# 32-column inverses in a chunked recurrence, its output normalised in the last head pair, and an output projection begun over them

## The reference, cut to what matters

```
def step(state, inp):                       # 256 steps, 16 heads of 64
    r_t, w_t, k_t, v_t, a_t, b_t = inp
    sa = einsum('bhvk,bhk->bhv', state, a_t)
    state = state * w_t + sa * b_t + v_t * k_t
    y_t = einsum('bhvk,bhk->bhv', state, r_t)
mean, var = mean(y), mean((y - mean)^2)     # over the 64 of a head
y = (y - mean) * rsqrt(var + 64e-5) * lnx_w + lnx_b
y = (y + sum(r * k * r_k) * v) * g
x = x + y @ w_o
```

## Time and profile before

| | us |
|---|---|
| median of 3 runs | 1403.82 (1401.42 to 1408.97) |
| the profiled execution's own time | 1402.62 |
| its span in the trace | 1400.4 |
| scores, projection of r, levels and steps of pair 0 to 3 | 99.3 to 322.4 |
| normalisation and output projection | 322.4 to 365.8 |

### The profile page before, as it was taken

One profiled execution on the slowest core, in us unless ns is written; L12 is line 12 of the kernel. 1 busy time (PEld: TensorE's weight loads), 2 busy tenths in 40 slices (PEclk: granted clock), 3 DMA queues, 4 the chain that ended last, 5 costly groups with the idle time before them and its releaser, 6 DMA issues.

```text
span 1400.4 us, 21886 instructions
## 1 busy us (share of the span) xinstructions
PE 1255.3 (90%) x9218; PEld 1167.3 (83%) x9218; DVE 940.1 (67%) x1298; ACT 630.4 (45%) x829; POOL 208.5 (15%) x139
## 2 busy tenths in 40 slices
PE   3998989887899999699888889999789887999995
PEld 3887878775899999696667888999789877999995
DVE  6767657544468874755864567774548835999994
ACT  4464343224443445456556564434442244544442
POOL 0000000000264442000000122210000001344431
PEclk9999999898999999899998999999899997999998
DMA  7440001000577764253322668785342213545530
GB/s 269 151 154 31 32 1 61 1 1 1 196 268 246 247 214 154 90 184 117 119 92 95 216 246 286 268 288 181 121 151 91 90 61 120 175 164 185 186 135 30
DMA packets 122656, 200.20 MB, mean 143 GB/s; under 512 B 3264, under 2 KB 111168, under 8 KB 112320
## 3 DMA queue, kind: packets, MB, share of 16 engines
q1 hardware_dynamic: 117664, 168.05, 35.7%
q0 software_dynamic: 3456, 25.17, 4.8%
q10 hardware_dynamic: 1440, 5.60, 1.1%
HBM read 197.75 MB, written 1.05 MB: 142 GB/s over the span
## 4 chain that ended last, share of the span: by engine, by line
PE 63%; DVE 24%; ACT 7%; issue 5%; DMA 0%; DVEq 0%; POOL 0%; ACTq 0%
PE bank L631 13%; PE bank L632 12%; PE bank L633 12%; DVE buf L2390 7%; DVE ring_r L1696 6%; PE bank L714 3%; PE bank L716 3%; PE bank L715 3%; ACT high L1173 2%; DVE work L1952 2%; PE bank L647 2%; PE bank L869 2%; DVE work L1948 2%; PE bank L857 2%; PE bank L1065 1%
## 5 line engine op out<-in xcount | busy, mean ns | idle before, releaser
L631 PE MATMUL bank<-part,high 128*128 128x256 f32 x1664 | 485.8, 292 | 66.6 <-DVE part L1703 61.5
L632 PE MATMUL bank<-part,high 128*128 128x256 f32 x1664 | 481.7, 289 | 0.0
L1696 DVE TENSOR_TENSOR ring_r<-ring,high 128x2048 fp32r<-128x2048 f32 (+1 forms) x155 | 342.9, 2221 | 206.3 <-ACT high L1173 204.0
L633 PE MATMUL bank<-part,ring_r 128*128 128x256 f32 x1664 | 481.1, 289 | 0.0
L631 PEld LDWEIGHTS bank<-part,high 128*128 128x128 f32 x1664 | 329.4, 198 | 75.3 <-issue 52.6
L632 PEld LDWEIGHTS bank<-part,high 128*128 128x128 f32 x1664 | 329.5, 198 | 0.3 <-issue 0.2
L633 PEld LDWEIGHTS bank<-part,ring_r 128*128 128x128 f32 x1664 | 329.1, 198 | 0.0
L1173 ACT ACTIVATE high<-ring 128x2048 fp32r<-128x2048 f32 x155 | 295.2, 1906 | 51.1 <-PE bank L633 40.9
L1623 POOL TENSOR_TENSOR ring_r<-ring,high 128x512 fp32r<-128x512 f32 x44 | 95.4, 2167 | 534.0 <-ACT high L1173 533.9
L714 PE MATMUL bank<-part,high 128*128 128x256 f32 x528 | 151.3, 287 | 9.2 <-POOL part L1617 4.9
L715 PE MATMUL bank<-part,high 128*128 128x256 f32 x528 | 150.1, 284 | 0.0
(11 more groups left out here) (260 smaller groups left out, 1580.9 us busy)
## 6 DMA issues: line engine op xcount, KB each, us to landing
ring<-in_wide SPq DMA_DIRECT2D x122, 1024.0 KB, 5.9
ring<-in_down SPq DMA_DIRECT2D x33, 1024.0 KB, 5.0
buf<-in_wide POOLq DMA_DIRECT2D x24, 1024.0 KB, 7.2
con<-in_cons SPq DMA_DIRECT2D x1, 1472.0 KB, 10.9
ring<-in_wide SPq DMA_DIRECT2D x2, 576.0 KB, 7.0
buf<-in_wide ACTq DMA_DIRECT2D x1, 1024.0 KB, 5.4
buf<-in_wide SPq DMA_DIRECT2D x1, 1024.0 KB, 5.3
buf<-in_ctx_t ACTq DMA_DIRECT2D x1, 1024.0 KB, 4.7
```

Source lines behind the costliest of these rows:

```text
L631: mm(bank, ah, bh, start=start, stop=False, skip_group_check=shared)
L632: mm(bank, ah, bl, start=False, stop=False, skip_group_check=shared)
L633: return mm(bank, al, bh, start=False, stop=stop, skip_group_check=shared)
L1696: v.tensor_tensor(low, raw, hi.bitcast(F32), ALU.subtract).then_inc(sem("unit_low"), 1)
```

## The change

**Levels 1 to 4** work on the blocks of the diagonal only. X of four 32x32 blocks is kept as a tile of 128 partitions by 32 columns (`x`, for four systems 128x128), and y and dx move 32 columns instead of 128, with a stationary matrix of 128x128 still: `near` (the scores inside the diagonal blocks) for y and the block-diagonal `xt` for dx. y now reads X as it is and dx reads it transposed, so the next y waits for the predicated copy alone (`x_ready`), and dx for the transposes (`xt_ready`). The transposes are four of 32x128 in place of one of 128x512. **Level 5** uses `far` (the scores between diagonal blocks, two small ScalarE copies of each group at level 1); its dx is eight matmuls in place of four, with 64 and 96 stationary columns, and TensorE's transposes at level 5 are gone. Small ScalarE copies (`left_diagonal`, `left_corner`) and two VectorE transposes build the operands of level 6. **Scores:** a fifth, small matmul in each of the 8 banks. **Setup of a pair:** VectorE has one more operation of 128x512 (`near`) and three more transposes for a group. **Pair 3:** ahead of its levels TensorE subtracts the mean of quarters 0 to 2 by one matmul each (`y_centre`), ScalarE squares and copies them, TensorE sums the squares after level 1, the Ln and Exp stand between the levels, and VectorE's operations for quarters 0 to 2 (`y_out`) stand before `st` and after it. **Projection:** TensorE does the first six of eight row tiles of units 0, 1 and 2, then the last two of each, then unit 3. The table of constants is 512 columns longer.

```diff
-        y_sq = buf[11]
+        y_sq = buf[1]
+        def chain_parts(g):
+
+            t = work[:, g % 2]
+            return t[:, 0, :], t[:, 1, :], t[:, 2, :], t[:, 3, 0:P], t[:, 3, P:2 * P]
+        def left_of(g):
+
+            return work[0:CH, g % 2, 3, 2 * P:4 * P].rearrange("p (j n) -> p j n", j=4)
...
+                def y_centre(j):
+                    for g in (2 * j, 2 * j + 1):
+                        wait_freed(pe, ("yt", g))
+                    bank = open_bank(("yc", j))
+                    close(mm(bank[:, :], const("centre"), piece(y_t, j), start=True, stop=True), ("yc", j))
+
+                def y_variance(j):
+                    pe.wait_ge(sem("y_sq"), j + 1)
+                    bank = open_bank(("yvar", j))
+                    close(mm(bank[:, :], const("head_sum"), piece(y_sq, j), start=True, stop=True), ("yvar", j))
+                def o_tiles(i, kts):
+                    w = arrived("o", i // 2, i % 2)
+                    bank = bank_of(("o", i)) if kts[0] else open_bank(("o", i))
+                    for kt in kts:
+                        wait_part("y", kt)
+                        for half in range(2):
+                            last = split_mm(bank[:, half * S:(half + 1) * S], [z[:, kt, half * P:(half + 1) * P] for z in w], tile_of("y", kt),
+                                            kt + half == 0, kt == KT - 1, shared=True)
+                    if kts[-1] == KT - 1:
+                        close(last, ("o", i))
...
-                                mm(bank[:, 0:P], at_, bt_, start=True, stop=True)
+                                mm(bank[:, 0:P], bt_, at_, start=True, stop=True)
+                                mm(bank[CH:P, 0:CH], at_[:, CH:P], bt_[:, 0:CH], start=True, stop=True)
...
+                    else:
+                        for j in range(p):
+                            y_centre(j)
...
-                                pe.wait_ge(sem(f"xt_ready{g % 2}"), SQUARE * (g // 2) + l)
+                                pe.wait_ge(sem(f"x_ready{g % 2}"), SQUARE * (g // 2) + l)
+                            if l == SQUARE:
+                                pe.wait_ge(sem(f"far_ready{g % 2}"), g // 2 + 1)
-                                    last = mm(bank[:, s_], scores[g % 2][:, j, 0:P], xt[:, s_], start=True, stop=True)
+                                    last = mm(bank[:, j * SQ:(j + 1) * SQ], (near if l < SQUARE else far)[:, s_], x[:, j * SQ:(j + 1) * SQ], start=True, stop=True)
...
+                            if l <= SQUARE:
+                                pe.wait_ge(sem(f"xt_ready{g % 2}"), SQUARE * (g // 2) + l)
+                            else:
+                                pe.wait_ge(sem(f"x_left{g % 2}"), g // 2 + 1)
                             for j in range(4):
-                                s_ = slice(j * P, (j + 1) * P)
-                                if what == "dx":
-                                    last = mm(bank[:, s_], y[:, s_], x[:, s_], start=True, stop=True)
+                                y_ = y[:, j * SQ:(j + 1) * SQ]
+                                if l < SQUARE:
+                                    last = mm(bank[:, j * SQ:(j + 1) * SQ], xt[:, j * P:(j + 1) * P], y_, start=True, stop=True)
+                                elif what == "dx":
+                                    mm(bank[0:CH, (4 + j) * SQ:(5 + j) * SQ], xt[:, j * P:j * P + CH], y_, start=True, stop=True)
+                                    last = mm(bank[0:P - SQ, j * SQ:(j + 1) * SQ], xt[:, j * P + SQ:(j + 1) * P], y_, start=True, stop=True)
                                 else:
-                                    last = mm(bank[0:CH, j * CH:(j + 1) * CH], x[0:CH, j * P:j * P + CH], y[0:CH, j * CH:(j + 1) * CH], start=True, stop=True)
+                                    last = mm(bank[0:CH, j * CH:(j + 1) * CH], left_of(g)[:, j, :], wide_y(g)[:, j * CH:(j + 1) * CH], start=True, stop=True)
...
-                                    s_ = slice(j * P, (j + 1) * P)
-                                    last = nc.tensor.transpose(bank[:, s_], x[:, s_], ident)
+                        elif l == 1:
+                            for j in range(p):
+                                y_variance(j)
...
-                for g in range(NG):
-                    wait_freed(pe, ("yt", g))
-                sums_over("ymean", const("head_sum"), y_t, lambda j: None)
-                sums_over("yvar", const("head_sum"), y_sq, lambda j: pe.wait_ge(sem("y_sq"), j + 1))
-                project("o", "y")
+                y_centre(3)
+                o_tiles(0, range(0, 6))
+                y_variance(3)
+                for i in (1, 2):
+                    o_tiles(i, range(0, 6))
+                for i in range(3):
+                    o_tiles(i, range(6, KT))
+                o_tiles(3, range(0, KT))
...
+                    far = squares(chain_parts(g)[1])
+                    own.go(act_(far[0:SQ, :, SQ:CH], scores[g % 2][0:SQ, :, SQ:CH], ACT.Copy))
+                    act_(far[CH:CH + SQ, :, CH + SQ:P], scores[g % 2][CH:CH + SQ, :, CH + SQ:P], ACT.Copy).then_inc(sem(f"far_ready{g % 2}"), 1)
...
+                    for b in range(2):
+                        r = slice(b * SQ, (b + 1) * SQ)
+                        own.go(act_(left_of(g)[r, :, r], x[r, :, :], ACT.Copy))
...
+                    act_(left_of(g)[SQ:CH, :, 0:SQ], bank_of(key)[SQ:CH, P:2 * P].rearrange("p (j n) -> p j n", j=4), ACT.Copy).then_inc(sem(f"x_left{g % 2}"), 1)
...
+                    wait_full(eng, key)
+                    act_(piece(y_sq, j), bank_of(key)[:, :], ACT.Square).then_inc(sem("y_sq"), 1)
+                    release(act_(piece(y_t, j), bank_of(key)[:, :], ACT.Copy), key)
...
+                            y_square(j)
+                        log_table()
...
-                            m, n = (P, 512) if l < LEV - 1 else (CH, 4 * CH)
-                            release(act_(work[0:m, g % 2, 3, 0:n], bank_of(key)[0:m, 0:n], ACT.Copy), key)
-                        if SQUARE <= l < LEV - 1:
+                            if l < LEV - 1:
+                                release(act_(chain_parts(g)[3], bank_of(key)[:, 0:P], ACT.Copy), key)
+                            else:
+                                release(act_(wide_y(g), bank_of(key)[0:CH, 0:4 * CH], ACT.Copy), key)
-                                release(act_(work[:, g % 2, 2, :], bank_of(key)[:, :], ACT.Copy), key)
+                                far_blocks(g)
+                        if l == SQUARE:
+                            for g in pair:
+                                left_diagonal(g)
+                            own.settle()
+                            for g in pair:
+                                left_corner(g)
...
+                        elif l <= 3:
+                            y_log(l - 1)
+                        else:
+                            y_root(l - 4)
...
+                        if not nxt and what in ("sa0", "sa1"):
+                            part_of("y", what == "sa1")
...
-                for j in range(4):
-                    eng.wait_ge(sem("y_centered"), j + 1)
-                    act_(piece(y_sq, j), piece(y_t, j), ACT.Square).then_inc(sem("y_sq"), 1)
-                rsqrt_of([(("yvar", j), piece(y_sq, j)) for j in range(4)], CH, eps_lnx, "y_root")
-                parts("y")
+                log_table()
+                y_square(3)
+                part_of("y", 2)
+                y_log(3)
+                y_root(3)
+                part_of("y", 3)
...
+                    def turned(g, back):
+
+                        xt, x = squares(chain_parts(g)[2]), squares(chain_parts(g)[4])
+                        for b in range(4):
+                            r = slice(b * SQ, (b + 1) * SQ)
+                            dst, src = (xt[r, :, r], x[r, :, :])[::-1 if back else 1]
+                            ins = v.transpose(dst, src)
+                            own.go(ins) if b < 3 else ins.then_inc(sem(f"{'x' if back else 'xt'}_ready{g % 2}"), 1)
...
-                        turned(g)
+                        eng.sem_inc(sem("scores_in"), 1)
+                        v.copy_predicated(squares(xt), spread(const("left_right"), [P, 4, P]).bitcast(I32), scores[g % 2][:, :, 0:P])\
+                            .then_inc(sem(f"xt_ready{g % 2}"), 1)
+                        own.go(v.tensor_tensor(squares(near), scores[g % 2][:, :, 0:P], spread(const("near"), [P, 4, P]), ALU.mult))
+                        eng.wait_ge(sem(f"xt_ready{g % 2}"), SQUARE * (g // 2) + 1)
+                        own.settle()
+                        turned(g, True)
...
+                                x = squares(chain_parts(g)[4])
+                                block = bank_of(key)[:, 0:P].rearrange("p (j n) -> p j n", j=4)
+                                v.copy_predicated(x, spread(const("joins", (l - 1) * SQ, SQ), [P, 4, SQ]).bitcast(I32), block).then_inc(sem(f"x_ready{g % 2}"), 1)
```

(34 more changed lines are left out.)

121 lines of the change are left out of this document (60 added, 61 removed).

## The result

The changed kernel takes 1468.95 us in the median of 4 runs (1468.44 to 1470.66), against 1403.90 for the kernel before beside it: 1.0458 times as long, 95% interval 1.0429 to 1.0486. The forecast was slower, 1429 in a range of 1388 to 1450: the direction held, the size didn't. The profiled execution's span is 1467.2 us in place of 1400.4, 66.8 more. TensorE is busy for 1340.1 us in place of 1255.3; VectorE and ScalarE hardly change. All of it lies ahead of the norm's root, which starts at 436.56 in place of 369.42, 67.1 later.

A forecast was written before the change was run, and what follows sets the result against it. It took a chain over three engines, TensorE nearly full, to bound the levels, and statistics the end. Terms 9 + 12 + 4 + 4 + 8 - 10.6 = +26.4 us on 1402.6 gave 1429, range 1388 to 1450.

The forecast's parts named there:

- The clock: TensorE in levels 1 to 6: expected to fall from 2.4 to 1.2 GHz some microseconds into the levels.
- The second rival: TensorE stays at 2.4 GHz in levels 2 to 4, making the kernel faster, 1381 us; chance 0.12.
- The price of 32 columns: Matmuls of levels 1 to 4: eight records cost 1.03 us at 2.4 GHz, 1.71 at 1.2, as for 64 columns.
- the first rival: Levels: TensorE falls to 1.2 GHz, but 32 columns take about 0.16 us a record, not 0.213; 1411 us, chance 0.10.
- Scores, +4: Score stage, all pairs: a fifth matmul in 8 banks, 16 records of 0.071 us, 1.1 a pair; +4.0 us (2 to 7).
- Levels 1 to 4, +12: Levels 1 to 4, all four pairs: +3.0 us each, mostly at 1.2 GHz after about 7 us.
- TensorE alone sets a level: Levels 1 to 4: other engines' work hides under the other group's matmuls; a level takes 4.1 us or 6.85 at 1.2 GHz.
- Levels 5 and 6, +16: Levels 5 and 6, all four pairs: 12.0 us against 7.7, +4.0 each, with dx at 0.14 a record.
- Steps, +4: Steps behind the levels inherit 1.2 GHz; pair 3 loses 0.7 to 7.7 us; +4.0 over all (0 to 10).
- The end, -10.6: Last y to the norm's root: 34.0 us against 46.6, less some 2 for 1.2 GHz carried in; -10.6 (-13 to -5).

## Why the forecast was right in direction and wrong in size

*The clock: right.* The step "I expect it at 1.2 GHz from some microseconds into the levels" stands in the rows after, and the runs with 64 and 128 columns show that the narrow matmuls do it. The second rival (the clock stays up) didn't come about; nor would it have given its 1381: with 128 columns (0.112 a record) and the clock at 1.00 levels 1 to 4 of pair 0 saved 0.2 us, not the 3.6 of its sum.

*The price of 32 columns: right at 1.2 GHz*, 0.213 a record as put down, and a level of four groups took 6.83 us as worked out; the first rival (0.16) fell. At 2.4 GHz it was 0.107 and not 0.129.

*Scores, +4: the step that failed.* "16 records of 0.071" took the price of a 64x64 record in a row of its like and added it to TensorE's time. The stage's own rows would have told otherwise: eight records in 0.55 us are 0.07 each only because two heads run side by side, and a matmul of another shape between them ends that. Measured: 0.55 us a bank and not 0.14, 4.4 us in pair 1. On top of it the clock fell in pair 2's scores (22.6 us at 0.62), which neither the kernel without the fifth matmul nor the two with another form or place shows; what in the longer stage did it wasn't tried. In all +25.3 against +5, half of the whole miss of 40.

*Levels 1 to 4, +12: mis-sized, with a term and a wait left out*, +21.2. The bound for a clock all low was +7.4 a pair, and pair 3 reached +8.5. The term left out is pair 3's three `y_variance`: the sum has `y_centre` but not these. In the changed kernel they hold TensorE for 5.3 us in level 1 at the low clock:

```profile
340.90 5.47 PE L839 MATMUL bank<-buf,con 128*128 128x512 f32 x6
346.16 1.06 PE L909 MATMUL bank<-work 128*128 128x32 f32 x6
```

The wait left out is level 3's. "TensorE alone sets a level" was right in level 4 at the low clock (6.83 us in every pair), and in pair 2 (26.18 busy of 26.24), but level 3 took 8.6 and 8.2 us in pairs 0 and 1. The trace before had it: its four levels take, from the first y of one to that of the next, 4.60, 4.98, 5.81 and 4.99, and the prediction read four equal periods and "1.7 for the next pair's key sum". At 2.4 GHz VectorE's four transposes stood in the way as well.

*Levels 5 and 6, +16: mis-sized*, +20.7. dx was priced at 0.14 a record, which fits like behind like (0.137), and took 0.203: the change between 64 and 96 columns at every matmul is the rest, 2 us a pair.

*Steps, +4: mis-sized*, +12.4. Pair 3 alone lost 10.8, where the prediction had 7.7 at most: its bound was pair 2's stretch at 0.69, and this one ran at 0.52 through all 25.2 us.

*The end, -10.6: right*, -12.5. The 34.0 us worked out from VectorE's and ScalarE's chain were 34.1, the same in every kernel with the new end; the 2 us for a low clock carried in didn't come (0.95 in this stretch). In the changed kernel, the chain that ended last has it so: the last low split of a weight unit, sum, square, sum of the norm, root.

```profile
432.32 1.76 DVE ring_r L1802
434.08 0.61 DVE resid L1836
...
435.39 1.15 PE bank L671 x4
436.56 0.47 ACT rstd L1249
```

What stays open is where exactly the clock falls. Each edit moved it to another place, sometimes by 6 us of time; what the runs show is which matmuls ran ahead of it, not a rule that gives the microsecond.

## What to carry to other kernels

Cutting the moving columns of a matmul from 128 to 32 saved next to nothing here while the stationary matrix stayed 128 wide (0.112 to 0.107 a record), and cost half of the clock; look at the granted clock of each stretch, and where it falls in a busy stretch, try to move more columns, even useless ones. A price per record taken from matmuls that run side by side isn't the price of one more of another shape in their midst: measure a stage by its period. Measure the period of each level too, and not their mean: the odd one holds the wait. Of a change in several parts, try the parts apart: here the new end with wider steps gives 0.985 of the time before, while no kernel with the new levels and scores beat the same kernel without them.

## What the hardware showed that was not expected

- 128 moving columns cost hardly more than 32 under 128 stationary ones: 16 records of y in 1.79 us against 1.71, both at 2.4 GHz; with 64 it was 1.73.
- The clock fell in a stretch in which TensorE was busy for 3.89 of 4.00 us moving 32 columns, and stayed at 0.50 for 28 us of work; with 128 columns the fall in the levels lasted 3.4 us.
- A 64x64 tile between 64x128 tiles cost 0.33 us a bank more than a 64x128 one in its place; eight 64x64 records together take 0.38 us.
- The stationary width counts at 1.2 GHz (0.110, 0.163, 0.213 us for 64, 96, 128 columns among their like); the first record behind a change between 64 and 96 takes 0.225 or 0.278.
- A transpose of 32x128 takes 0.33 us, a quarter of 1.30, against 0.71 for one of 128x512 with sixteen times the elements.
